# When the square sums of a norm are issued: two bursts at the first slot against one inside the second

## The reference

```
def rms_norm(x, g):
    y = x * rsqrt(mean(x * x, axis=-1) + EPS)
    return y * g
...
h = rms_norm(x, ffn_norm[i])
x = x + conv_ffn(h, ...)
```

## Time and profile before

| | |
|---|---|
| median of 3 runs | 1327.38 us (1326.45 to 1327.82) |
| span of the profiled execution | 1324.4 us |
| median less span | 3.0 us |
| PE busy | 1296.3 us (98%) |
| POOL busy | 1006.1 us (76%) |
| ACT busy | 682.9 us (52%) |
| DVE busy | 637.0 us (48%) |

### The profile page before, as it was taken

One profiled execution on the slowest core, in us unless ns is written; L12 is line 12 of the kernel. 1 busy time (PEld: TensorE's weight loads), 2 busy tenths in 40 slices (PEclk: granted clock), 3 DMA queues, 4 the chain that ended last, 5 costly groups with the idle time before them and its releaser, 6 DMA issues.

```text
span 1324.4 us, 27666 instructions
## 1 busy us (share of the span) xinstructions
PE 1296.3 (98%) x10976; PEld 1247.4 (94%) x10976; DVE 637.0 (48%) x1163; ACT 682.9 (52%) x944; POOL 1006.1 (76%) x793
## 2 busy tenths in 40 slices
PE   6999999999999999999999999999999999999999
PEld 6889999999988889999999978999999999999998
DVE  8994465555555748455565574211113455311112
ACT  7725643444666756443457565434446566543342
POOL 1327888888777659888887794988887766988885
PEclk9999999999999999999999999999999999999999
DMA  6305675545535235555454532555554433555530
GB/s 269 129 33 181 169 250 191 185 172 181 191 134 185 101 126 183 178 188 188 172 178 160 193 128 96 192 192 179 174 185 167 160 126 120 187 178 187 190 127 32
DMA packets 33879, 217.07 MB, mean 164 GB/s; under 512 B 3683, under 2 KB 7428, under 8 KB 8196
## 3 DMA queue, kind: packets, MB, share of 16 engines
q1 hardware_dynamic: 30096, 211.14, 45.1%
q10 hardware_dynamic: 3700, 4.75, 1.4%
HBM read 213.26 MB, written 2.62 MB: 163 GB/s over the span
## 4 chain that ended last, share of the span: by engine, by line
PE 85%; DVE 6%; ACT 6%; issue 2%; POOL 1%; DMA 0%; DVEq 0%; SPq 0%; ACTq 0%; POOLq 0%
PE up L1568 19%; PE up L1569 18%; PE up L1570 18%; PE acc L1568 7%; PE acc L1570 6%; PE acc L1569 6%; DVE opnd L972 2%; PE side L1795 2%; PE up L1703 1%; PE acc L1761 1%; ACT w_hi L503 1%; ACT opnd L641 1%; PE side L1576 1%; PE up L1834 1%; PE acc L1933 0%
## 5 line engine op out<-in xcount | busy, mean ns | idle before, releaser
L413 POOL TENSOR_TENSOR w_lo<-ring,w_hi 128x512 fp32r<-128x512 f32 x748 | 955.4, 1311 | 235.7 <-ACT w_hi L503 231.8
L1568 PE MATMUL up<-opnd,w_hi 128*128 128x256 f32 x2064 | 592.3, 287 | 3.7 <-DVE opnd L972 1.5
L1569 PE MATMUL up<-opnd,w_lo 128*128 128x256 f32 x2064 | 583.9, 283 | 0.0
L1570 PE MATMUL up<-opnd,w_hi 128*128 128x256 f32 x2064 | 583.8, 283 | 0.0
L503 ACT ACTIVATE w_hi<-ring 128x2048 fp32r<-128x2048 f32 x188 | 358.9, 1910 | 264.4 <-PE up L1570 202.7
L1568 PEld LDWEIGHTS up<-opnd,w_hi 128*128 128x128 f32 x2064 | 395.6, 192 | 16.1 <-issue 13.1
L1569 PEld LDWEIGHTS up<-opnd,w_lo 128*128 128x128 f32 x2064 | 395.8, 192 | 1.3 <-issue 1.0
L1570 PEld LDWEIGHTS up<-opnd,w_hi 128*128 128x128 f32 x2064 | 395.7, 192 | 0.0
L1568 PE MATMUL acc<-opnd,w_hi 128*128 128x256 f32 x784 | 223.0, 284 | 1.2 <-DVE x L1218 1.2
L1569 PE MATMUL acc<-opnd,w_lo 128*128 128x256 f32 x784 | 221.8, 283 | 0.0
L1570 PE MATMUL acc<-opnd,w_hi 128*128 128x256 f32 x784 | 221.8, 283 | 0.0
(11 more groups left out here) (296 smaller groups left out, 1421.3 us busy)
## 6 DMA issues: line engine op xcount, KB each, us to landing
ring<-in_stream SPq DMA_DIRECT2D x197, 1024.0 KB, 4.9
bias_rows<-mix ACTq DMA_DIRECT2D x1, 1536.0 KB
mix<-in_s_b SPq DMA_DIRECT2D x1, 1024.0 KB, 5.6
x<-in_x SPq DMA_DIRECT2D x1, 1024.0 KB, 7.7
mix<-in_s_c SPq DMA_DIRECT2D x1, 1024.0 KB, 11.7
mix<-bias_rows ACTq DMA_DIRECT2D x1, 1024.0 KB, 5.4
out_x<-x SPq DMA_DIRECT2D x8, 128.0 KB, 1.7
mix<-in_p ACTq DMA_DIRECT2D x2, 256.0 KB, 3.4
```

Source lines behind the costliest of these rows:

```text
L413: ins = nc.gpsimd.tensor_tensor(w_l[:, cols], ring[:, r, cols], w_h[:, cols].bitcast(f32), ALU.subtract)
L1568: MM(o, l_hi, r_hi, start=start, stop=False, skip_group_check=True)
L1569: MM(o, l_lo, r_hi, start=False, stop=False, skip_group_check=True)
L1570: return MM(o, l_hi, r_lo, start=False, stop=stop, skip_group_check=True)
```

## The change

The two bursts of the first slot are taken out. All sixteen matmul instructions are issued as one burst after the first K step of the second slot. The fold moves from the first to the third step of that slot, and the token factors from the fourth to the sixth. The arithmetic is the same. The calls inside the first slot go from `up_slot`, `token_slot`, `diff_half` and `stick_half`; the last lines of the diff show `up_slot`'s.

```
-            def square_sums(h):
-                c.wait("sq_ready", KT // 2)
-                for q in range(4):
-                    ins = MM(aux[1][QUAD * q:QUAD * q + QUAD, 0:T], ones[:, 0:QUAD], sq[:, 4 * h + q],
-                             start=(h == 0), stop=(h == 1), tile_position=(0, QUAD * q), skip_group_check=True)
-                if h:
-                    c.up(ins, "ssq")
+            def square_sums():
+                c.wait("sq_ready", KT)
+                for h in range(2):
+                    for q in range(4):
+                        ins = MM(aux[1][QUAD * q:QUAD * q + QUAD, 0:T], ones[:, 0:QUAD], sq[:, 4 * h + q],
+                                 start=(h == 0), stop=(h == 1), tile_position=(0, QUAD * q), skip_group_check=True)
+                c.up(ins, "ssq")
...
             def between(k, fold, tokens):
                 if fold and k == 0:
+                    square_sums()
+                if fold and k == 2:
                     all_sums()
-                if tokens and k == 3:
+                if tokens and k == 5:
                     token_rstd(tokens)
...
-                    if sums and j == KT // 2 - 1:
-                        square_sums(0)
                     between(k, fold, tokens)
                 c.up(ins, "mm_done")
-                if sums:
-                    square_sums(1)
```

More of the change, by code:

```diff
@@ L1596, in between, with up_slot @@
                 if fold and k == 0:
+                    square_sums()
+                if fold and k == 2:
                     all_sums()
-                if tokens and k == 3:
+                if tokens and k == 5:
                     token_rstd(tokens)
-            def up_slot(name, s, i=None, fresh=False, sums=False, fold=False, tokens=0, order=range(KT)):
+            def up_slot(name, s, i=None, fresh=False, fold=False, tokens=0, order=range(KT)):
                 slot_ready(s, i)
@@ L1652, in token_slot @@
                                     k == 0 and t == 0, k == KT - 1)
-                    if fresh and k == KT // 2 - 1:
-                        square_sums(0)
                     between(k, fold, tokens)
                 c.up(ins, "mm_done")
-                if fresh:
-                    square_sums(1)
             def down_tile(s, ops, m, k, first, last):
@@ L1853, in ffn @@
                 assert used[0] == BANK[f"ffn{l}"]
-                up_slot(name, S, fresh=True, sums=True, order=order)
+                up_slot(name, S, fresh=True, order=order)
                 up_slot(name, S + 1, fold=True)
@@ L1884, in ple @@
                 for g in range(3):
-                    up_slot(f"ple{l}", S + g + 1, fresh=(g == 0), sums=(g == 0), fold=(g == 1))
+                    up_slot(f"ple{l}", S + g + 1, fresh=(g == 0), fold=(g == 1))
                 s, name = S + 4, f"ple{l}"
@@ L1922, in diff_half @@
                     c.up(ins, "mm_done")
-                if i == 0:
-                    square_sums(half)
             def diff_stats(n):
```

## The result

The changed kernel takes 1331.07 us (median of 6, 1330.99 to 1332.29) against 1326.95 us for the kernel before in the same runs (median of 6, 1326.45 to 1327.82): 4.1 us more. The ratio is 1.0032, with a 95% interval from 1.0022 to 1.0043, so it is slower by more than the 0.2% that can be told. The forecast was 1330.9.

A forecast was written before the change was run, and what follows sets the result against it. TensorE (PE), busy 98% of the span, was taken as the bound. ffn0/ffn3 -0.64, ple0/ple1 +0.56, ffn1/ffn2/even +1.32, even's bank +0.25, odd +0.17, kvq +1.87: +3.5 on 1327.38 gives 1330.9 us; range 1328.6 to 1332.6.

The forecast's parts named there:

- The price of a burst: Each norm on PE: two bursts of eight cost 1.52 us, one of sixteen 1.20, saving 0.32 where PE can use it.
- First slots that wait: kvq, ffn1, even, ffn2: PE waits for the last low tile, gains nothing there and pays 0.44 us in the second slot.
- ple0 and ple1: Second slot waits for POOL's weights: PE keeps 0.16 us of 0.76 and pays 0.44, so +0.28 each.
- The hidden wait: ple's fifth slot: PE waits some 1.2 us for weights, costed at nothing because PE has about 1.9 us to spare later.
- The fold and the token factors: Token matmuls come 1.87 us later; slack in plain norms, but kvq's wait for L1318 grows to 2.6 and kvq loses 1.87.
- the rival that the stage gives the wait back: kvq: ACT or a later wait absorbs the 1.43 us beyond PE's own 0.44; sum +2.1, 1329.5 us; chance 0.18.
- even and odd: Third-slot banks: even +0.25 beside its 0.44; odd +0.02 from lost saving and 0.15 for bank and fourth slot's weights.
- even's bank: even's third slot: DVE frees the bank at 739.90, PE is there at 739.79; a new wait of 0.25 us.
- The sum: All nine norms together: +3.5 us on the median 1327.38, giving 1330.9, or +0.27%.
- The rival that every burst saved counts: All nine norms: PE has its 0.32 us in each, so 1327.38 - 2.9 = 1324.5 us; chance 0.07.
- The rival of a dearer ple: ple's later POOL low parts: +0.8 us in kvq and even, or the slot wait shows; +4.7 to +5.1, 1332.3; chance 0.14.

The follow-up runs named there:

- experiment 2: Kernel before with the sixteen matmuls merged at the end of the first slot, fold and token factors at their old steps: 1328.13 us against 1327.13 (1.0007).
- experiment 7: Kernel before with one burst of sixteen at the first slot's end in ffn0, ple0, ple1 and ffn3 alone: 1326.21 us against 1326.99 (1.0013).
- experiment 1: Kernel before with each norm's first burst left out and nothing in its place: 1323.61 us against 1326.99 (ratio 0.9974).
- experiment 3: Kernel before, two bursts kept, only the fold moved after the third and token factors after the sixth step: 1329.63 us against 1327.13 (1.0021).
- experiment 4: Changed kernel with the token factors after the fifth instead of the sixth step: 1329.79 us against 1327.13 for the kernel before (1.0033).
- experiment 5: Changed kernel with the token factors after the seventh instead of the sixth step: 1334.54 us against 1327.13 for the kernel before (1.0067).
- experiment 6: Kernel before with the token factors after the third instead of the fourth step, bursts and fold unchanged: 1326.63 us against 1326.99 (0.9999).
- the second series: The changed kernel run once more for its profile, against the kernel before: 1332.53 us (median of 7) against 1327.13 (1.0061).
- experiment 8: As experiment 7, plus kvq, even, ffn2's second burst inside PE's wait, earlier tokens in kvq and odd, earlier fold in even: 1325.22 us against 1326.99 (0.9998).
- experiment 9: As experiment 8, with odd's token factors back after the fourth step: 1325.04 us against 1327.13 for the kernel before (1.0005).
- experiment 10: The kernel of experiment 9 run once more against the kernel before: 1324.10 us (median of 11) against 1327.26 (0.9977).

## Why the prediction was right, point by point

*The price of a burst* was right: 1.20 forecast for sixteen, 1.19 measured, and the 0.33 us appear wherever PE could use them (experiments 2 and 7).

*First slots that wait* was right, and experiment 1 shows it alone: zero in kvq, ffn1, even and ffn2 for a burst of 0.76. The detail that I gave for the profile was off: I said that the wait for L972 would grow to some 6 us. It is 3.0, and 3.5 with the one listed under L641. A burst taken out shows in the list as 0.48 us and not as 0.76 (experiment 1); and in ple PE is held earlier, at the weights of the second and fifth slots (POOL, 2.6 in four waits), so that the last waits of kvq and even have shrunk from 0.98 to 0.76 us.

*ple0 and ple1* were forecast at +0.28 and came to +0.40. Two terms were undersized. The hidden wait isn't wholly hidden: experiment 3, which moves nothing else in these norms, has +0.07. The remaining 0.05 lies at the second slot: PE begins it 0.87 us earlier than before, where I had reckoned with 0.82, but I had also counted as saved the 0.10 us that the start behind a burst comes late. The start behind a held one comes as late (353.92 and 354.14 above).

*The fold and the token factors* was right in its main term. kvq was forecast at +1.87 and has +1.83 with the clock up; the wait is 2.60 where the forecast said 2.6. The chain hangs on the tokens, not on the fold (experiments 4 to 6, where the fold stays), and ACT doesn't catch up. So the rival that the stage gives the wait back is refuted by experiment 3 (+1.45 where it asked for nothing).

*even and odd* were undersized by 0.15 and 0.13. even's bank costs 0.40 in place of 0.25: 0.33 at the start that waits and 0.07 at the one behind it. odd pays 0.05 up to the second slot's burst and fold (forecast 0.02), 0.18 at the third slot's bank and the fourth's weights (forecast 0.15), and 0.07 at a later wait for DVE (L2177) that the forecast didn't have.

*The sum,* +3.5, stands against +3.93 in the profile with the clock up, +4.1 between the medians and +5.4 in the second series: the small terms above all erred to one side. That 1330.9 lies within 0.2 us of the first measured median is partly luck: I added the sum to 1327.38, the median of three executions, and the six have 1326.95. The rival that every burst saved counts would have been faster by 2.9 us, and experiment 1 refutes its condition; the drain on a change of tiling mode that the Trainium skill (TensorEngine Tiling (Array Packing), section Tiling Modes) speaks of agrees with the trace, where the start of a burst follows after 0.21 us and that of the fold, which keeps the mode, after 0.12; but the rule speaks of PE alone. The rival of a dearer ple falls too: the last low tile came 0.15 us before PE's last step as ever, at its short length of 0.48 us, and even's has the same length.

## What to carry to other kernels

Before taking work off the busiest engine, look for its next wait: what stands ahead of a wait for another engine's result is free already, and moving it behind that wait makes it cost its full price. And a wait costs more than its idle time: count the late start behind it too, here 0.07 to 0.10 us each. The better edit is the other way round, to put work of the busy engine into its waits (experiments 8 to 10: -2.6 us by the trace with nearly the same instructions).

A step that looks like slack on one engine may stand at the head of another engine's list. The token factors were not late for anything that reads them in kvq; but ACT waits for them in order, and all its later work moved with them.

## What the runs showed of the hardware

A wait of PE of 2.6 or 3.0 us let its granted clock fall to the lower of its two levels (1.2 GHz) in two of five profiles, at a price of 1.5 us each. The same wait in another execution of the same kernel did not. So such a wait makes a kernel's time not only longer but uneven, and a single profile can hold a term that the median doesn't have: the first profile of the changed kernel did. PE's one other wait of this length, 3.0 to 3.1 us for ACT's L578 at 14 us, stands in all 14 profiles, and in eight the granted clock falls there, in the kernel before to 0.50 from 13.5 to 16.5 us; in the other six the record of the clock begins only at about 19 us.

A start of PE that was held makes the next one late as well: in all 17 waits of L1568 that the changed kernel's first profile lists with more than 0.1 us, the next start follows after 0.19 to 0.22 us in place of 0.12.

Taking the token factors one K step (0.7 us) earlier in odd made PE lose 0.45 and 0.49 us (experiments 6 and 8) at L942 in the attention part, some 34 us later. That it is tied to the tokens is shown (experiments 8 to 10); the path is open.
